# One sparse-attention, mLSTM and mixture-of-experts layer: the choice rounds divided over other units, the first modulation in halves on two engines, and the shared expert's silu released by the gate product alone

## What is computed

```python
mod = jax.nn.silu(c) @ w_ada[l] + b_ada[l]
sh1, sc1, gt1, sh2, sc2, gt2 = jnp.split(mod[:, None, :], 6, axis=-1)
h = rms_norm(x, g_mix_pre[l]) * (1.0 + sc1) + sh1      # the modulated input
proj = h @ w_in[l]                                      # first projection
...
# dsa_attention, for a block of 128 queries
rel = jax.nn.relu(jnp.einsum("bqhd,bsd->bqhs", iqb, ik))
score = jnp.einsum("bqh,bqhs->bqs", iwb, rel)
score = jnp.where(admissible[None], score, -jnp.inf)
_, idx = lax.top_k(score, k_top)                        # k_top = 128 of up to 512 keys
logits = jnp.einsum("bqhd,bqkd->bhqk", qb, kg) * scale
p = jax.nn.softmax(logits, axis=-1)
out = jnp.einsum("bhqk,bqkd->bqhd", p, vg)
...
# channel part: routed experts, and the shared expert
shared = (jax.nn.silu(hf @ ws_gate) * (hf @ ws_up)) @ ws_down
```

## Time and profile before

| | us |
|---|---|
| median of 3 runs | 1045.74 |
| lowest and highest of the 3 | 1045.54, 1047.65 |
| the profiled execution, whole | 1045.84 |
| its span, from first to last instruction | 1044.0 |
| PE busy in it | 984.9 (94%) |
| DVE busy | 913.2 (87%) |
| ACT busy | 685.2 (66%) |
| POOL busy | 231.3 (22%) |

### The profile page before, as it was taken

The page is one execution under the profiler, slowest core; times in us unless marked ns, Lnnn a source line. Parts: engine busy times, 40 slices in busy tenths (PEclk is TensorE's granted clock), DMA queues, the critical chain, the costliest instruction groups (busy, mean ns, idle before and its releaser), DMA issues.

```text
span 1044.0 us, 15335 instructions
## 1 busy us (share of the span) xinstructions
PE 984.9 (94%) x5065; PEld 777.3 (74%) x5066; DVE 913.2 (87%) x1268; ACT 685.2 (66%) x736; POOL 231.3 (22%) x144
## 2 busy tenths in 40 slices
PE   0899999988999999999999999999999999999996
PEld 0898889756546647888888887888888887888884
DVE  3888899878576757999999999999999999999986
ACT  2524365456222137888888888888888888888873
POOL 0000000100000031233323333342433342333320
PEclk9899999899999999999999999999999999999999
DMA  9877210240593539999999999999999999999934
GB/s 355 288 252 235 84 42 1 92 172 1 197 379 148 218 101 389 358 379 367 378 381 370 377 371 372 367 373 376 371 368 370 361 381 369 386 381 375 319 86 162
DMA packets 89333, 296.25 MB, mean 284 GB/s; under 512 B 17185, under 2 KB 29645, under 8 KB 79821
## 3 DMA queue, kind: packets, MB, share of 16 engines
q1 hardware_dynamic: 69476, 259.18, 63.8%
q0 software_dynamic: 18304, 33.60, 13.4%
q10 hardware_dynamic: 1514, 2.97, 0.8%
HBM read 289.39 MB, written 39.32 MB: 315 GB/s over the span
## 4 chain that ended last, share of the span: by engine, by line
PE 49%; issue 7%; DVE 5%; ACT 2%; DVEq 0%
PE ps L2117 29%; PE ps L2173 11%; PE ps L2107 5%; ACT w_gate_up_hi L1832 2%; PE ps L2135 1%; DVE xT_lo L1967 1%; DVE w_down_lo L1985 1%; PE ps L2125 1%; PE ps L2182 1%; DVE pick L1945 1%; PE ps L2191 1%; PE ps L2100 0%; DVE w_gate_up_lo L1963 0%; DVE uT_lo L1976 0%; DVE u L1972 0%
## 5 line engine op out<-in xcount | busy, mean ns | idle before, releaser
L1629 POOL DMA_INDIRECT y_rows<-yb,row_numbers x62 | 147.5, 2378 | 294.4 <-DMA y_rows<-yb,row_numbers 268.0
L1963 DVE TENSOR_TENSOR w_gate_up_lo<-side,w_gate_up_hi 128x2048 fp32r<-128x2048 f32 x64 | 146.5, 2289 | 11.8 <-ACT w_gate_up_hi L1832 11.6
L1963 DVE TENSOR_TENSOR w_gate_up_lo<-main,w_gate_up_hi 128x2048 fp32r<-128x2048 f32 x64 | 146.4, 2287 | 5.6 <-ACT w_gate_up_hi L1832 5.5
L2117 PE MATMUL ps<-w_gate_up_hi,xT_hi 128*128 128x512 f32 x512 | 144.5, 404 | 6.6 <-DVE xT_lo L1967 5.6
L2117 PE MATMUL ps<-w_gate_up_hi,xT_lo 128*128 128x512 f32 x512 | 137.4, 390 | 0.0
L2117 PE MATMUL ps<-w_gate_up_lo,xT_hi 128*128 128x512 f32 x512 | 137.0, 389 | 0.0
L1832 ACT ACTIVATE w_gate_up_hi<-side 128x2048 fp32r<-128x2048 f32 x64 | 122.3, 1912 | 5.9 <-PE ps L2117 4.0
L1832 ACT ACTIVATE w_gate_up_hi<-main 128x2048 fp32r<-128x2048 f32 x64 | 122.5, 1914 | 2.9 <-PE ps L2117 2.4
L2117 PEld LDWEIGHTS ps<-w_gate_up_hi,xT_hi 128*128 128x128 f32 x512 | 91.3, 188 | 29.1 <-issue 12.8
L2117 PEld LDWEIGHTS ps<-w_gate_up_hi,xT_lo 128*128 128x128 f32 x512 | 96.1, 188 | 21.0
L2117 PEld LDWEIGHTS ps<-w_gate_up_lo,xT_hi 128*128 128x128 f32 x512 | 96.1, 188 | 20.4
(11 more groups left out here) (323 smaller groups left out, 1804.6 us busy)
## 6 DMA issues: line engine op xcount, KB each, us to landing
side<-in_w_exp_gate SPq DMA_DIRECT2D x60, 512.0 KB, 8.4
side<-in_w_exp_up SPq DMA_DIRECT2D x60, 512.0 KB, 10.1
main<-in_w_exp_gate SPq DMA_DIRECT2D x60, 512.0 KB, 8.3
main<-in_w_exp_up SPq DMA_DIRECT2D x60, 512.0 KB, 9.9
side<-in_w_ada SPq DMA_DIRECT2D x20, 1024.0 KB, 7.7
main<-in_w_exp_down SPq DMA_DIRECT2D x16, 1024.0 KB, 7.6
maskb<-in_w_exp_down SPq DMA_DIRECT2D x16, 1024.0 KB, 7.5
side<-in_w_exp_down SPq DMA_DIRECT2D x16, 1024.0 KB, 7.5
```

Of the source, the lines that this page charges most:

```text
L1629: return pool.indirect_dma_start(out=G.y_sums, out_offset=bass.IndirectOffsetOnAxis(ap=sidx[:, n:n + 1], axis=0), in_=yb[:, slot, :], in_o ...
L1963: nc.vector.tensor_tensor(wlo[:, half], src, whi[:, half].bitcast(F32), ALU.subtract).then_inc(s_wlo, 1)
L2117: ins = nc.tensor.matmul(ps[0:CAP, 2 + slot, :], xp[:, HALF * half + c, :], wp[:, half, c].rearrange("p m f -> p (m f)"), start=half == 0 ...
```

## The change

Three places are changed.

At the first projection, the scale columns are summed in two halves of four (`sum_modulation(1, range(NT))`, then the rest once DVE has read the first), and DVE makes `modB` and `modA` of each half on its own (`mod_columns`). Slices 2 and 3 of `hf` are made by DVE (`modulate_h`) and the six others by ACT. The transposition of slice 7 moves into the first item's first part, between c = 3 and c = 4 (`turn_last`), and the first item begins when two slices of each engine are there, no longer four of ACT's. DVE's `low_part(0)` moves from ahead of the modulation to between the roundings of slices 6 and 7.

In the attention units the four rounds of the choice are divided: maxima at u = 4, 6, 8, 9, replacements at u = 5, 7, 9, 10, and the closing steps at u = 11.

In the shared expert the silu waits for the gate product alone, and DVE's multiplication waits for the up product itself.

```diff
--- before.py
+++ after.py
@@ -211,6 +211,8 @@
+        s_hfd = sem("h_modulated_by_vector")
+        s_modr = sem("mod_sums_read")
@@ -240,6 +242,7 @@
+        BY_ACT, BY_DVE = (0, 1, 4, 5, 6, 7), (2, 3)
@@ -330,8 +333,8 @@
 
-            act.wait_ge(s_modd, 1)
-            for c in range(KC):
+            for c in BY_ACT:
+                act.wait_ge(s_modd, c // NT + 1)
                 act.wait_ge(s_xT, c + 1)
                 nc.scalar.activation(hf[:, c, :], ps[:, c, :], ACT.Identity, bias=modB[:, c:c + 1],
                                      scale=modA[:, c:c + 1]).then_inc(s_hf, 1)
@@ -491,14 +494,41 @@
+            def mod_columns(n):
+
+                c = slice(NT * n, NT * (n + 1))
+                dve.wait_ge(s_mod, n + 1)
+                nc.vector.tensor_tensor(modB[:, c], ps[:, 7, NT * n:NT * (n + 1)], bcol[:, 0, c], ALU.add)
+                nc.vector.scalar_tensor_tensor(modA[:, c], ps[:, 7, KC + NT * n:KC + NT * (n + 1)], 1.0, bcol[:, 1, c],
+                                               ALU.add, ALU.add).then_inc(s_modr, 1)
+                dve.wait_ge(s_modr, n + 1)
+                nc.vector.tensor_tensor(modA[:, c], modA[:, c], gpre[:, c], ALU.mult).then_inc(s_modd, 1)
+
+            def modulate_h(c):
+
+                dve.wait_ge(s_modd, 1)
+                dve.wait_ge(s_xT, c + 1)
+                nc.vector.tensor_scalar(hf[:, c, :], ps[:, c, :], modA[:, c:c + 1], modB[:, c:c + 1],
+                                        ALU.mult, ALU.add).then_inc(s_hfd, 1)
+
+            def h_high(c):
+
+                if c in BY_ACT:
+                    dve.wait_ge(s_hf, BY_ACT.index(c) + 1)
+                else:
+                    dve.wait_ge(s_hfd, BY_DVE.index(c) + 1)
+                nc.vector.tensor_copy(hhi[:, c, :], hf[:, c, :]).then_inc(s_hhi, 1)
+
+            mod_columns(0)
+            modulate_h(2)
+            h_high(0)
+            modulate_h(3)
+            h_high(1)
+            mod_columns(1)
+            for c in range(2, KC - 1):
+                h_high(c)
             low_part(0)
-            dve.wait_ge(s_mod, 1)
-            step(nc.vector.tensor_tensor(modB[:, :], ps[:, 7, 0:KC], bcol[:, 0, :], ALU.add))
-            step(nc.vector.scalar_tensor_tensor(modA[:, :], ps[:, 7, KC:2 * KC], 1.0, bcol[:, 1, :], ALU.add, ALU.add))
-            nc.vector.tensor_tensor(modA[:, :], modA[:, :], gpre[:, :], ALU.mult).then_inc(s_modd, 1)
-            for c in range(KC):
-                dve.wait_ge(s_hf, c + 1)
-                nc.vector.tensor_copy(hhi[:, c, :], hf[:, c, :]).then_inc(s_hhi, 1)
+            h_high(KC - 1)
             for c in range(KC):
                 dve.wait_ge(s_hhi, c + 1)
                 nc.vector.tensor_tensor(hlo[:, c, :], hf[:, c, :], hhi[:, c, :].bitcast(F32), ALU.subtract).then_inc(s_hlo, 1)
@@ -623,17 +653,16 @@
             pe.wait_ge(s_in, 16 * 8)
             nc.tensor.transpose(ps[:, 6, 0:44], colrows[:, :], ident[0:44, 0:44]).then_inc(s_cols, 1)
 
-            def sum_modulation(s):
-
-                for c in range(KC):
+            def sum_modulation(s, columns):
+
+                for c in columns:
                     ins = nc.tensor.matmul(ps[:, 7, s * KC + c:s * KC + c + 1], acc[:, s, c:D:KC], k[:, K_ONES:K_ONES + 1],
                                            start=True, stop=True)
                 if s:
                     ins.then_inc(s_mod, 1)
 
-
             pe.wait_ge(s_ada_used, len(ADA) // 2)
-            sum_modulation(0)
+            sum_modulation(0, range(KC))
             pe.wait_ge(s_xn, NT + 1)
             pe.wait_ge(s_colsd, 1)
             for c in range(KC - 1):
@@ -641,20 +670,29 @@
                     ins = nc.tensor.transpose(ps[:, c, i * P:(i + 1) * P], xn[:, i, c:D:KC], ident)
                 ins.then_inc(s_xT, 1)
             pe.wait_ge(s_ada_used, len(ADA))
-            sum_modulation(1)
-            pe.wait_ge(s_modd, 1)
-            for i in range(NT):
-                ins = nc.tensor.transpose(ps[:, KC - 1, i * P:(i + 1) * P], xn[:, i, KC - 1:D:KC], ident)
-            ins.then_inc(s_xT, 1)
+            sum_modulation(1, range(NT))
+            pe.wait_ge(s_modr, 1)
+            sum_modulation(1, range(NT, KC))
+
+            def turn_last():
+
+                pe.wait_ge(s_modr, 2)
+                for i in range(NT):
+                    ins = nc.tensor.transpose(ps[:, KC - 1, i * P:(i + 1) * P], xn[:, i, KC - 1:D:KC], ident)
+                ins.then_inc(s_xT, 1)
+
             PARTS = ((hhi, whi), (hlo, whi), (hhi, wlo))
 
             def project_first():
                 w = width(ITEMS[0])
                 pe.wait_ge(s_whi, 1)
-                pe.wait_ge(s_hf, NT)
+                pe.wait_ge(s_hf, 2)
+                pe.wait_ge(s_hfd, 2)
                 for j, (hp, wp) in enumerate(((hhi, whi), (hhi, wlo), (hlo, whi))):
                     wt = wp[:, 0, 0:KC * w].rearrange("p (c n) -> p c n", c=KC)
                     for c in range(KC):
+                        if j == 0 and c == NT:
+                            turn_last()
                         pe.wait_ge((s_hhi, s_wlo, s_hlo)[j], (c + 1, 1, c + 1)[j])
                         for i in range(NT):
                             ins = nc.tensor.matmul(ps[:, i, 0:w], hp[:, c, i * P:(i + 1) * P], wt[:, c, :],
@@ -692,7 +730,7 @@
             project(1)
             project(2)
             project(3, [0])
-            pe.wait_ge(s_hf, KC)
+            pe.wait_ge(s_hf, len(BY_ACT))
             pe.wait_ge(s_rope, 1)
             for i in range(NT):
                 if i >= 2:
@@ -806,7 +844,7 @@
         UNITS = [(h, i) for i in range(NT) for h in range(HEADS)]
-        LAST_ROUNDS = (5, 6, 7, 8)
+        LAST_MAX, LAST_REPLACE = (4, 6, 8, 9), (5, 7, 9, 10)
@@ -947,6 +985,14 @@
+            def choose_max():
+
+                step(nc.vector.max(G.top8, G.last_left))
+
+            def choose_replace():
+
+                step(nc.vector.match_replace(G.last_left, G.top8, G.last_left, FMIN))
+
             def choose_last():
 
                 step(nc.vector.max(G.top8, G.last_left))
@@ -1024,9 +1070,11 @@
                 if u < HEADS + 2:
                     norm_head(u - 2)
                 invert(u - 1)
-                if u in LAST_ROUNDS:
-                    choose_last()
-                if u == LAST_ROUNDS[-1] + 1:
+                if u in LAST_REPLACE:
+                    choose_replace()
+                if u in LAST_MAX:
+                    choose_max()
+                if u == LAST_REPLACE[-1] + 1:
                     step(nc.vector.tensor_tensor(G.last_left, G.last_left, maskb[:, NT - 1, :], ALU.is_equal))
                     step(nc.vector.tensor_scalar(maskb[:, NT - 1, :], G.last_left, NEG, None, ALU.mult))
                 if u >= HEADS + 2 and (u - 2) % HEADS == 0:
@@ -1209,7 +1257,8 @@
         s_h2Td = sem("h2_T_copied")
-        s_gu = sem("shared_gate_up")
+        s_gate = sem("shared_gate")
+        s_gu = sem("shared_up")
@@ -1316,7 +1365,7 @@
             nc.scalar.activation(sco[:, :, :], ps[:, 4, 0:NT * E_N].rearrange("p (i e) -> p i e", i=NT), ACT.Sigmoid).then_inc(s_sco, 1)
             act.wait_ge(s_used, 8)
             for f in range(FC):
-                act.wait_ge(s_gu, f + 1)
+                act.wait_ge(s_gate, f + 1)
                 nc.scalar.activation(sg[:, f, :], ps[:, f, :], ACT.Silu).then_inc(s_sg, 1)
 
         @block.vector
@@ -1462,6 +1511,7 @@
 
             def multiply(f):
                 dve.wait_ge(s_sg, f + 1)
+                dve.wait_ge(s_gu, f + 1)
                 nc.vector.tensor_tensor(uT[:, f, :], sg[:, f, :], ps[:, 2 + f, :], ALU.mult).then_inc(s_u, 1)
 
             multiply(0)
@@ -1502,8 +1552,8 @@
                 for c in range(KC):
                     ins = nc.tensor.matmul(ps[:, 2 * m + f, t0:t1], (wg, wu)[m][:, c, f * P:(f + 1) * P], h2T[:, c, t0:t1],
                                            start=c == 0, stop=c == KC - 1)
-                if m == 1:
-                    ins.then_inc(s_gu, 1)
+                if t1 == SEQ:
+                    ins.then_inc((s_gate, s_gu)[m], 1)
 
             def sum_rows(r0, r1):
                 for r in range(r0, r1):
```

## The result

The changed kernel takes 1040.39 us, the median of 7 executions, against 1045.74 for the kernel before in the same comparison. The ratio is 0.9941, 95% interval 0.9927 to 0.9954, a gain of 4.8 to 7.6 us. Some executions of any kernel here take 15 us or more longer than the rest, in the two that were profiled (e5 and e15) within the expert stage; they are left out of ratios and means, so the ratio is not the quotient of the two medians, and of e5's and e15's profiles only the part ahead of the experts is read. The profiled execution took 1039.33 us, its span 1037.5. The forecast was 1041.5, its range 1039.8 to 1043.9. The time lies inside the range, but the gain, 6.5 us between the two profiled executions, is 2.2 us more than the sum of 4.3. Six executions of each in this comparison have means 5.7 us apart.

A forecast was written before the change was run, and what follows sets the result against it. The prediction took PE to bound the kernel, DVE close behind and setting the pace in attention units 5 to 11. Its terms, 1.8 + 1.9 + 0.6 = 4.3 us, gave 1041.5 us, range 1039.8 to 1043.9.

The forecast's parts named there:

- The front: First projection: halved sums, DVE's slices and the later low part start the first item's second part 1.8 us earlier.
- a clock that follows the start of the item by 4.1 us: First projection: PE's clock rises 4.1 us after the first item begins, at 45.5 us.
- The rival of a late clock: First projection: the clock rises as late as before, the edit gives 1.0 us, not 1.8; 1042.3 us, chance 0.15.
- The units: Attention units: dividing the choice rounds brings unit 9's inversion 1.97 us earlier; gain taken as 1.9 us.
- The slack of 0.4 us: Attention units: DVE's 4.46 us of work up to unit 11's inversion fits PE's 4.85 us, by 0.4 us.
- the change wins only by what it puts behind the inversion of unit 9: Attention units: only the last replacement and closing steps, moved behind that inversion, pay; 0.79 + 1.18 = 1.97 us.
- with DVE dense: Attention units: DVE taken as working almost without gaps, busy 15.97 of 16.6 us from 240.0 to 256.6.
- The silu: Shared expert: the second silu is done earlier, so DVE multiplies from 374.8 us; gain 0.6 us.
- The step that failed: Stretches beyond the edits: gains reach the end undiminished, and the expert stage's length is left as it is.
- more than forecast: Pause ahead of the attention units: an earlier arrival may spare a clock fall, at most half of 3.4 us; 1039.8, chance 0.05.
- The base: Whole kernel before: median 1045.74 us, profiled execution 1045.84, from which the gain was subtracted.
- Slower: First item: the clock stays low through all 96 products, 6.0 us slower less 2.5; 1049.3 us, chance 0.05.

The follow-up runs named there:

- e5: The changed kernel, but ACT makes all eight modulated slices, as before the change; ratio to the kernel before 0.9947.
- e15: The kernel before run once more, unchanged, for a second profile; ratio to the kernel before 1.0003.
- e12: The changed kernel with choice-round maxima at units 4, 5, 6, 7 and replacements at 5, 6, 7, 10; ratio to the kernel before 0.9960.
- e7: The changed kernel with all four choice rounds ahead of unit 9's inversion, only the closing steps behind; no ratio, units 37.88 us in its profile.
- e8: The changed kernel with three unused products in PE's two pauses ahead of the first turned unit; 1040.6 us, ratio to the kernel before 0.9938.
- e13: The kernel before with 11 more products (1.33 us) ahead of the attention stage; ratio to the kernel before 0.9998.

## Where the prediction was right, and where it failed

Means over all profiles with the piece as before and as changed, the added products taken off:

| stretch | as before | as changed | gain | forecast |
|---|---|---|---|---|
| to the attention stage | 164.1 (8; 163.8 to 164.8) | 162.1 (8; 161.7 to 162.5) | 2.1 | 1.8 |
| its first part, by the front, nothing added | 32.1 (5) | 31.05 (6) | 1.05 | 0 |
| the units | 38.8 (7) | 36.6 (8) | 2.2 | 1.9 |
| routing | 104.86 | 104.30 | 0.56 | 0.6 |
| experts, by the front | 668.2 (7) | 667.7 (9) | 0.5 | 0 |

Sum 6.4, and 6.4 is measured between the means of executions. The close agreement is partly luck: in the second and the last row single executions differ by more than the gain.

- **The front**, 1.8: right in size and in its steps, within 0.4 us at each place. DVE's modulation was mis-sized, 0.81 us and not 0.69, and shorter steps beside it made up for that. My one fixed number was wrong in kind: "a clock that follows the start of the item by 4.1 us". In 18 profiles the rise came 3.1 to 5.7 us after it. That is the spread of this term: the second part begins 13.2 to 14.2 us after the first one-column product with the old front and 11.2 to 11.7 with the changed one. The rival of a late clock, a rise near 48.4 us as in the kernel before, did not occur: with the changed front or a variant of it the latest rise was at 47.0.
- **The units**, 1.9: right in size, by the step that was named (1.97 forecast, 1.98 measured, at the inversion of unit 9). The slack of 0.4 us behind it was there: DVE came to the logits of unit 12 without a wait and waited 0.36 us for those of unit 13. But "the change wins only by what it puts behind the inversion of unit 9" was too short: e12 puts the same work there and loses 1.5 of the 1.9. The premise "with DVE dense" was taken from one stretch; it holds only because the rounds are divided.
- **The silu**, 0.6: right.
- **The step that failed** is the one ahead of the sum and the one behind it: that what lies beyond the edits keeps its length, read from one execution. That execution had 6.8 us at half clock in the attention stage (all of 202.00 to 208.50 in the row above), worth 1.9 us, which I did not look for: it lay between the stretches I had read, to 200 and from 232 us, and PE has no wait in it. The cost is less than the 3.4 us by which the half clock could lengthen PE's work, because with the full clock PE waits 0.8 and 0.5 us for DVE in the same place. The rival "more than forecast" had the right idea, a fall spared by an earlier arrival, but at the pause ahead of the units, where it is worth 0.5 us, and at a chance of 0.05. Its true place was the stage's start and its price 1.9 us. Its share in the mean is an estimate: 1.05 us by the table, 0.4 to 0.6 by the distances (three of eight against six or seven of ten, at 1.9 us each). The rest, 0.5 us in the table, is the experts: 667.1 to 667.4 or 668.5 to 669.1, in seven of sixteen profiles the longer, six of these with the clock fallen at 376 to 403 us. Whether the change has a part in that is open.
- **The base**: three executions gave 1045.74 for the kernel before, 73 give a mean of 1046.75. The base was 1.0 us too low and the gain 2.1 too small, and the two errors partly cancel in the time of 1041.5. From a base of 1046.75 the same sum gives 1042.45 and a range from 1040.8 up, which 1040.39 misses. That the time lies inside the range is luck.
- **Slower**, by a clock that stays low through the first item: no profile came near; the latest rise was at 49.7 us, in e15, which has the old front.

No kernel run here beats the changed one by more than its executions differ.

## What to carry to other kernels

Before summing edits, list every stretch of the profile in which the granted clock is at half, what PE does there and who sets the pace: what is spared is worth much where PE is dense (1.9 us of 6.8) and little where another engine leads (0.5 of 3.4). Take each such stretch as a coin whose odds an edit ahead can change, and price both sides, since one profile shows only one. And when work is moved off an engine that paces another, write down each deadline of the other. It is not enough that the total ahead of one deadline is right: a bad spread before it (e12), or the next deadline after it (e7), can take the gain back.

## What the runs showed of the hardware

- Behind a pause of PE of 0.91 us, followed by products of four rows, the clock fell to half for 3.4 or 6.8 us in 10 of 18 profiles, though PE was busy by the profile both before and after the pause. Which of the two, the pause or the thin products, matters was not tested. Ahead of the units it fell for 3.4 us or more around idle times of PE of 0.94 and 1.85 us, in 17 of 18 profiles; three products in these (e8) kept it up.
- Whether the fall at the attention stage came went with the time from a rise some 152 us earlier: falls up to 152.49 us, none from 152.62 to 153.07, falls again from 154.00. Adding 1.33 us of work left the mean time where it was, within 1.3 us (e13).
- DVE's `tensor_scalar` with two operands per partition, 512 columns from PSUM, takes 0.81 us; the multiplication of two tensors of that size, one of them in PSUM, takes 0.69. The Trainium skill (VectorE: DVE Perf Modes, Why PSUM operands drop a tier) has float data from PSUM at the single rate. Against 0.43 us for the rounding from SBUF, 0.81 agrees with that; why it is also longer than 0.69 no run shows.
